# Per-head norm, rotation and key copies carried out in four rounds inside the projection of the second block

## What is computed

```python
x = swiglu_half_step(x, ...); h_ctx = swiglu_half_step(h_ctx, ...)
hx, hc = modulate(rms_norm(x, g1), ...), modulate(rms_norm(h_ctx, g1), ...)
px, pc = hx @ w_in, hc @ (w_in[:, Q_W:] if last else w_in)
qa, qb, ka, kb = rms_norm(heads(...), qk_norm_g[l, ...])   # each head of 64 by itself
qb, kb = apply_axial_rope(qb), apply_axial_rope(kb)        # tokens only, not the context
out = neighbourhood_attention(qa, ka, va, ...), windowed_gqa_attention(qb, kb, vb, ...)
x = x + gate * (out @ w_out)
x = swiglu_half_step(x, ...)
```

## Time and profile before

| | us |
|---|---|
| median of three runs | 2911.91 |
| lowest, highest of them | 2911.59, 2916.3 |
| the profiled execution | 2916.71 |
| its span, first to last instruction | 2914.9 |

### The profile page before, as it was taken

One profiled execution on the slowest core, in us unless ns is written; L12 is line 12 of the kernel. 1 busy time (PEld: TensorE's weight loads), 2 busy tenths in 40 slices (PEclk: granted clock), 3 DMA queues, 4 the chain that ended last, 5 costly groups with the idle time before them and its releaser, 6 DMA issues. The chain is left out here.

```text
span 2914.9 us, 39615 instructions
## 1 busy us (share of the span) xinstructions
PE 2634.1 (90%) x15379; PEld 2218.6 (76%) x15379; DVE 1756.6 (60%) x3178; ACT 1082.2 (37%) x2062; POOL 226.3 (8%) x169
## 2 busy tenths in 40 slices
PE   4768998798997899998999889999899998989899
PEld 4747997777997688886845668888688886856899
DVE  6567776558776666546648475554565444647654
ACT  2333543344443333223217333322333323326553
POOL 2000100000100210001000020000110000100110
PEclk8867998878998999999979999999999999889999
DMA  8923774824765244432710124433344433720453
GB/s 287 273 94 120 256 250 155 243 64 145 234 223 180 86 131 131 140 119 78 231 52 1 53 93 145 144 123 115 98 142 130 155 121 100 216 72 30 143 174 133
DMA packets 355667, 413.96 MB, mean 142 GB/s; under 512 B 25755, under 2 KB 292676, under 8 KB 355416
## 3 DMA queue, kind: packets, MB, share of 16 engines
q1 hardware_dynamic: 353326, 404.37, 43.6%
q0 software_dynamic: 800, 4.63, 0.5%
q10 hardware_dynamic: 1354, 2.43, 0.2%
HBM read 409.78 MB, written 5.27 MB: 142 GB/s over the span
## 5 line engine op out<-in xcount | busy, mean ns | idle before, releaser
L644 DVE TENSOR_TENSOR weight_lo<-raw_weights,weight_hi 128x512 fp32r<-128x512 f32 x1024 | 777.6, 766 | 936.3 <-ACT weight_hi L1180 925.7
L1180 ACT ACTIVATE weight_hi<-raw_weights 128x512 fp32r<-128x512 f32 x1024 | 633.3, 629 | 1332.1 <-PE bank L852 1188.0
L852 PE MATMUL bank<-H_hi,weight_hi 128*128 128x256 f32 (+1 forms) x2832 | 972.2, 343 | 118.6 <-POOL H_lo L810 80.5
L852 PE MATMUL bank<-H_lo,weight_hi 128*128 128x256 f32 (+1 forms) x2832 | 954.0, 337 | 0.0
L852 PE MATMUL bank<-H_hi,weight_lo 128*128 128x256 f32 (+1 forms) x2832 | 953.8, 337 | 0.0
L852 PEld LDWEIGHTS bank<-H_hi,weight_hi 128*128 128x128 f32 x2832 | 555.1, 196 | 197.0 <-issue 119.8
L852 PEld LDWEIGHTS bank<-H_hi,weight_lo 128*128 128x128 f32 x2832 | 555.4, 196 | 50.9
L852 PEld LDWEIGHTS bank<-H_lo,weight_hi 128*128 128x128 f32 x2832 | 556.9, 197 | 48.8 <-issue 0.5
L1475 DVE SCALAR_TENSOR_TENSOR ada_partial<-raw_weights,silu_c,ada_partial 128x512 f32<-128x512 f32 x616 | 441.6, 744 | 1.3 <-DVE ada_partial L1475 0.2
L852 PE MATMUL bank<-hidden_hi,weight_hi 128*128 128x256 f32 (+1 forms) x1056 | 360.0, 341 | 3.5 <-DVE weight_lo L644 3.5
L852 PE MATMUL bank<-hidden_hi,weight_lo 128*128 128x256 f32 (+1 forms) x1056 | 355.1, 336 | 0.0
(11 more groups left out here) (170 smaller groups left out, 2079.0 us busy)
## 6 DMA issues: line engine op xcount, KB each, us to landing
raw_weights<-in_w_ada_dram SPq DMA_DIRECT2D x120, 1024.0 KB, 5.3
raw_weights<-in_w_ffn_up_dram SPq DMA_DIRECT2D x88, 1024.0 KB, 5.2
raw_weights<-in_w_ffn_in_dram SPq DMA_DIRECT2D x44, 1024.0 KB, 5.3
raw_weights<-in_w_ffn_down_dram SPq DMA_DIRECT2D x32, 1024.0 KB, 5.1
raw_weights<-in_w_in_dram SPq DMA_DIRECT2D x18, 1024.0 KB, 8.1
raw_weights<-in_w_ffn_out_dram SPq DMA_DIRECT2D x16, 1024.0 KB, 7.7
raw_weights<-in_w_in_ab_dram SPq DMA_DIRECT2D x12, 1024.0 KB, 9.1
raw_weights<-in_w_in_cd_dram SPq DMA_DIRECT2D x12, 1024.0 KB, 8.2
```

Of the source, the lines that this page charges most:

```text
L644: eng.tensor_tensor(WL[:, p.g % SPLIT, 0:p.kt * CW].rearrange("p (t n) -> p t n", n=CW), raw_ap(ch.n, ch.kt, CW)[:, p.k0:p.k0 + p.kt, :], ...
L852: return pe.matmul(o, w, x, start=start, stop=stop, skip_group_check=True)
L1180: act.activation(WH[:, p.g % SPLIT, 0:p.kt * CW].rearrange("p (t n) -> p t n", n=CW), raw_ap(ch.n, ch.kt, CW)[:, p.k0:p.k0 + p.kt, :], ACT ...
```

## The change

The stage `qk_norm` is gone as a stage. Its work is done in four rounds inside the projection, at places that a table fixes: after piece j of item i. The items come in another order, kv first, then k, q and v. The head sums of a round go to four strips of 32 partitions of one bank, from squares that ScalarE now takes out of PSUM; the root and the reciprocal are made once per round; spreads, rotations and copies use two banks in turn. Only the first four items host ada chunks, and the four items of the output projection host one each. The loads of the attention stage come in five parts (34 of them), with five more (tables for the spreads, rotations and copies) ahead of the first. The forget columns are loaded and split in the setup, and have no chunk in the ring.

```diff
-    c["head_cols"] = (half[:, None] + 24 == np.arange(50)[None, :]).astype(f)
-    c["head_rows"] = (np.arange(26)[:, None] == (2 * np.arange(13)[:, None] + half[None, :]).reshape(1, -1)).astype(f)
+    c["head_sum"] = (half[:, None] == np.arange(32)[None, :] // 16).astype(f)
+    m = np.zeros((P, P), f)
+    for r in range(P):
+        if r % 16 == 0:
+            m[r] = half == r % 32 // 16
+    c["head_spread"] = m
...
+    FRAW = region("forget_raw", [P, KC, 8])
...
-    HEAD_ROWS = PR[0:26, :, :].rearrange("p j n -> p (j n)")
+    SPREAD = PR[:, 0, 0:P]
+    SQUARES = [T1[:, 0, :], T1[:, 1, :], T2[:, 0, :], T2[:, 1, :]]
...
+    ROUNDS = ((12, 8, 9), (10, 11, 4, 5), (6, 7, 0, 1), (2, 3))
+    ROUND_END = (3, 7, 11, 13)
+    QK_AT = {(2, 1): (("sums", 0),), (2, 2): (("recip", 0),),
+             (3, 1): (("spread", 12), ("spread", 8)), (3, 3): (("spread", 9),),
+             (4, 0): (("rope", 12),), (4, 1): (("sums", 1),), (4, 2): (("recip", 1),),
+             (5, 0): (("spread", 10), ("spread", 11)), (5, 1): (("spread", 4), ("spread", 5)),
+             (5, 3): (("dup", 0), ("dup", 1)),
+             (6, 0): (("rope", 4), ("rope", 5)), (6, 1): (("sums", 2),), (6, 2): (("recip", 2),),
+             (7, 0): (("neighbour", 0),), (7, 1): (("spread", 6), ("spread", 7)),
+             (7, 2): (("spread", 0), ("spread", 1)), (7, 3): (("sums", 3),),
+             (8, 0): (("recip", 3), ("rope", 6)), (8, 1): (("rope", 7),), (8, 2): (("spread", 2), ("spread", 3))}
...
+        all_hosted = len(ADA) if len(ADA) == sum(ADA_CHUNKS) else None
+        add("proj", hosted=all_hosted, n=n, groups=groups, ada=ada, gate=gate, half=False, hidden=False, first=first,
...
-                st.items.append(Item(what=what, chunk=chunk("f", view(w), 0, KC, c0, 8), grp=None, host=None, n=n))
+                st.items.append(Item(what=what, chunk=None, grp=None, host=None, n=n))
...
-            [(0, ("q", 0)), (256, ("q", 2)), (512, ("q", 4)), (768, ("q", 6)), (1024, ("k", 0)),
-             (1280, ("k", 2)), (1536, ("v", 0)), (1792, ("v", 256)), (2048, ("kv",))], n, 8, T if last else n, 2 + l)
-        add("bias", what="na", layer=l, take=bias_in.take(16 * 39))
-
-        tiles = [(i, 2 * T) for i in (12, 8, 9, 10, 11)] + [(i, T if last else n) for i in (4, 5, 6, 7, 0, 1, 2, 3)]
-        add("qk_norm", layer=l, items=tiles, sq=qn_sq.take(13), sums=qn_sums.take(13), mm=qn_mm.take(13),
-            root=qn_root.take(1), out=qn_out.take(13), rmm=rope_mm.take(7), ro=rope_out.take(7),
-            q_in=state["q_in"], bias_in=bias_in.total)
-        state["normed"] = (qn_out.total, rope_out.total)
+            [(2048, ("kv",)), (1024, ("k", 0)), (1280, ("k", 2)), (512, ("q", 4)), (768, ("q", 6)), (0, ("q", 0)),
+             (256, ("q", 2)), (1536, ("v", 0)), (1792, ("v", 256))], n, 4, T if last else n, 2 + l)
+        add("bias", what="na", layer=l, take=bias_in.take(16 * 34))
+        state["normed"] = qn_read.total
...
-        w_out(a["w_out_2"][l], n2, 2 + l, 5, False, 0)
+        w_out(a["w_out_2"][l], n2, 2 + l, 5, False, 4)
...
-                tiles += [(HEAD_ROWS[:, 0:13 * P], c["head_rows"]), (COS[:, :], c["cos"]), (SIN[:, :], c["sin"]),
-                          (NEIGH[:, :], c["neg_neighbour"]), (WINDOW[:, :, :].rearrange("p q k -> p (q k)"), c["neg_window"]),
-                          (dup[0][:, :], c["dup0"]), (dup[1][:, :], c["dup1"])]
+                if part == 0:
+                    for dst, src in ((SPREAD, c["head_spread"]), (COS[:, :], c["cos"]), (SIN[:, :], c["sin"]),
+                                     (dup[0][:, :], c["dup0"]), (dup[1][:, :], c["dup1"])):
+                        sp.dma_start(dst, src).then_inc(spread_in, 16)
+                tiles += [(NEIGH[:, :], c["neg_neighbour"]), (WINDOW[:, :, :].rearrange("p q k -> p (q k)"), c["neg_window"])]
...
+                    parts = 7 if s.layer < 2 else 5
+                    if 2 <= s.items.index(it) < 2 + parts:
+                        bias(after, s.items.index(it) - 2, parts)
...
+            pool.dma_start(FRAW[:, :, :], view(a["w_in_cd"][0])[:, :, 3 * D:3 * D + 8]).then_inc(fg_in, 16)
...
+                if hook:
+                    hook(i)
...
+        def qk_norm(s, i, j):
+            for what in QK_AT.get((i, j), ()):
+                kind, t = what
+                if kind == "sums":
+                    if t:
+                        pe.wait_ge(qn_root.sem, s.root + t)
+                    for k, tile in enumerate(ROUNDS[t]):
+                        pe.wait_ge(qn_sq.sem, s.sq + ROUND_END[t] - len(ROUNDS[t]) + k + 1)
+                        w = s.rows[tile]
+                        mm(B_STAT[32 * k:32 * k + 32, 0:w], head_sum[:, :], SQUARES[k][:, 0:w], True, True
+                           ).then_inc(qn_sums.sem, 1)
+                elif kind in ("spread", "rope", "dup"):
+                    pe.wait_ge(qn_read.sem, s.take[what] - 1)
+                    o = B_T[s.take[what] % 2]
+                    if kind == "spread":
+                        (r, k), w = place(t), s.rows[t]
+                        pe.wait_ge(spread_in, 16 * 5 * (s.layer - 1))
+                        pe.wait_ge(qn_rstd.sem, s.rstd + r + 1)
+                        rows = slice(32 * k, 32 * k + 32)
+                        ins = mm(o[:, 0:w], SPREAD[rows, :], RB[rows, 0:w], True, True)
+                    elif kind == "rope":
+                        pe.wait_ge(qn_read.sem, s.take["spread", t] + 1)
+                        ins = mm(o[:, 0:T], rotate[:, :], qk_tile(t)[:, 0:T], True, True)
+                    else:
+                        pe.wait_ge(qn_read.sem, s.take["rope", 12] + 1)
+                        ins = mm(o[:, :], dup[t][:, :], KB[:, 4, :], True, True)
+                    ins.then_inc(qn_mm.sem, 1)
...
-                    pe.wait_ge(forget_used, 1)
+                    pe.wait_ge(fg_lo, 1)
...
+            act.wait_ge(fg_in, 16)
+            act.activation(FH[:, :, :], FRAW[:, :, :], ACT.Copy).then_inc(fg_hi, 1)
...
+        def qk_squares(s, it):
+            pair = PAIR[it.grp.n % 2]
+            for j, t in enumerate(item_tiles(it)):
+                (r, k), w = place(t), s.rows[t]
+                if r:
+                    act.wait_ge(qn_sums.sem, s.sums + ROUND_END[r - 1])
+                act.activation(SQUARES[k][:, 0:w], pair[j][:, 0:w], ACT.Square).then_inc(qn_sq.sem, 1)
+        def qk_roots(s, i, j):
+            for kind, r in QK_AT.get((i, j), ()):
+                if kind == "sums":
+                    rows = slice(0, 32 * len(ROUNDS[r]))
+                    act.wait_ge(qn_sums.sem, s.sums + ROUND_END[r])
+                    if r:
+                        act.wait_ge(qn_mm.sem, s.mm["spread", ROUNDS[r - 1][-1]] + 1)
+                    act.activation(RB[rows, :], B_STAT[rows, :], ACT.Sqrt, bias=EPS[rows, 1:2], scale=1.0 / HD
+                                   ).then_inc(qn_root.sem, 1)
...
+            dve.wait_ge(fg_hi, 1)
+            dve.tensor_tensor(FL[:, :, :], FRAW[:, :, :], FH[:, :, :].bitcast(F32), ALU.subtract).then_inc(fg_lo, 1)
+            dve.wait_ge(fg_lo, 1)
...
+        def qk_norm(s, i, j):
+            for what in QK_AT.get((i, j), ()):
+                kind, t = what
+                if kind == "recip":
+                    rows = slice(0, 32 * len(ROUNDS[t]))
+                    dve.wait_ge(qn_root.sem, s.root + t + 1)
+                    dve.reciprocal(RB[rows, :], RB[rows, :]).then_inc(qn_rstd.sem, 1)
+                elif kind == "neighbour":
+                    dve.wait_ge(bias_in.sem, s.bias_in)
+                    blocks = BT[:, :].rearrange("p (b k) -> p b k", k=T)
+                    chain.link(dve.scalar_tensor_tensor(out=blocks, in0=blocks, scalar=-1.0,
+                                                        in1=NEIGH[:, None, :].broadcast_to([P, 16, T]), op0=ALU.mult,
+                                                        op1=ALU.add))
+                elif kind != "sums":
+                    o = B_T[s.take[what] % 2]
+                    dve.wait_ge(qn_mm.sem, s.mm[what] + 1)
+                    if kind == "spread":
+                        x, w = qk_tile(t), s.rows[t]
+                        k = 1 + 4 * (s.layer - 2) + (0 if t < 4 else 2 if t < 8 else 1 if t < 12 else 3)
+                        ins = dve.scalar_tensor_tensor(out=x[:, 0:w], in0=x[:, 0:w], scalar=E_COLS[:, k:k + 1],
+                                                       in1=o[:, 0:w], op0=ALU.mult, op1=ALU.mult)
+                    elif kind == "rope":
+                        x = qk_tile(t)[:, 0:T]
+                        dve.tensor_tensor(o[:, 0:T], o[:, 0:T], SIN[:, :], ALU.mult)
+                        chain.link(dve.tensor_tensor(x, x, COS[:, :], ALU.mult))
+                        ins = dve.tensor_tensor(x, x, o[:, 0:T], ALU.add)
+                    else:
+                        ins = dve.tensor_copy(KB[:, 5 + t, :], o[:, :])
+                    ins.then_inc(qn_read.sem, 1)
...
```

(36 more changed lines are left out.)

112 lines of the change are left out of this document (26 added, 86 removed).

## The result

The changed kernel takes **2865.2 us** (median of 4, 2863.3 to 2866.0) where the kernel before takes 2913.4 on the same chip: a ratio of **0.9834, 95% interval 0.9819 to 0.9850**. It is 48 us faster, where 79 were forecast; the range, 2815 to 2858, misses it.

The account below looks back on a forecast made before the run. TensorE, busy nine tenths of the span, was taken to bound the kernel. Pass A -32.6, B -35.6, forget -11.0 and setup +0.5 summed to -78.7 us, giving 2833 us on the median's scale; 8-in-10 range 2815 to 2858.

Parts of the forecast that it names:

- Serial stage (1): Behind each projection of the second block: the one-engine-at-a-time stage goes, -49.0 us in pass A, -41.1 in B.
- Matmuls in the projection (2): Sums, spreads, copies and rotations put on TensorE, small neighbours overlapping: 15.5 us added in pass A, 11.9 in B.
- the rival that they run one after the other: Small matmuls in the projection don't overlap: pass A pays 11.1 us more, B 7.9; 2849 us, chance 0.15.
- Waits (3): TensorE waits in the projection for VectorE's results: 2.4 us in pass A, 5.3 in B.
- The rival of a wait in all eight rounds: VectorE comes late and TensorE waits the 3.34 us reciprocal in every round: 2858 us, chance 0.10.
- kv first (4): kv moved under the modulation at the projection's start, mostly hidden: -2.9 us in pass A, -8.2 in B.
- The bound I wrote and didn't use: For moving kv to the projection's start: kv wholly at half clock, +10 us in each pass.
- The rival on the clock: Many short waits let TensorE's clock fall to 0.50 in both projections, costing 175 us: 3008 us, chance 0.03.
- Hosting (5): Ada chunks 4 to 7 moved to output projection: weight waits -5.1, closings -0.9 in B; output projection +1.4 A, +2.5 B.
- step 3: Its VectorE finding: 81 us of work in pass A's stage of over 100, with four ada chunks, so it doesn't bound.
- Forget (7): First block: without the forget columns' ring slot, TensorE's wait for forget_lo goes, -11.0 us, bounds -3 and -14.
- setup (8): A load of 1,024 short pieces in GpSimd's queue and two 64-column instructions: +0.5 us, bounds 0 and 5.

Follow-up runs that it names:

- experiment 4: Kernel before with one edit, kv moved to the head of the second block's projection items, serial stage kept: 2934.6 us, ratio 1.0060.
- experiment 2: Changed kernel, kv still first, with eight idle 512-column f32 matmuls filling TensorE's wait for the first H_lo tile: 2832.0 us, ratio 0.9714.
- experiment 10: Kernel before with only the forget columns done as in the changed kernel: 2904.2 us, ratio 0.9972.
- experiment 5: Kernel before with v (0) as the first item of the second block's projection: 2914.9 us beside 2917.7, single run.
- experiment 6: Changed kernel with kv's twelve 128-column token matmuls per H tile made six of 256 columns, output partly wrong: 2840.6 us beside 2920.4, single run.
- experiment 1: Changed kernel with its first two items exchanged, k (0, 1) first and kv second: 2845.7 us, ratio 0.9760.
- experiment 3: Changed kernel, wait ahead of the first H_lo tile filled with only four idle 512-column matmuls: 2872.3 us beside 2917.7, single run.
- experiment 7: Changed kernel, wait ahead of the first H_lo tile filled with 32 idle 128-column matmuls: 2830.0 us beside 2920.4, single run.

## Why the prediction was wrong, step by step

- **Serial stage (1).** Right: all 90 us are gone. Behind each projection the clock is still at 0.50 for 3.4 us, where I had forecast no such stretch; it is small.
- **Matmuls in the projection (2).** Right: 1.06 for three or four sums and 1.13 for a pair against 1.07; the rival that they run one after the other is refuted by the rows shown.
- **Waits (3).** Fewer than I had: 0.2 us in pass A for my 2.4, 2.8 in pass B for my 5.3, of which 2.0 for round 1's reciprocal at (5, 0), where I had 1.8. The rival of a wait in all eight rounds is refuted. What the step lacked is the price behind a wait: the 2.0 us one is followed by some 10 us at half clock, up to 5 us that I put at nothing.
- **kv first (4).** This is the step that failed. I wrote "At the half clock of that stretch kv falls behind for the first tiles and then runs 2.04 a tile", which took for granted that the clock comes back under kv as it did under q in pass A. It did not: kv's end came 37.9 us after the reciprocal in both passes, not 25.8, and k's first piece cost 4.0 us more in A, 2.9 in B. Booked: -2.9 and -8.2. By experiment 4 the edit alone costs 14.0 and 6.8 us instead, 16.9 and 15.0 worse than booked, beside the 15.9 and 19.4 by which the passes miss the forecast. The rest of B's is about the size of the half clock behind its wait.
- **The bound I wrote and didn't use.** The same step named "kv wholly at half clock (+10 each)". With it the sum is 2833 + 12.9 + 18.2 = 2864 us; 2865.2 were measured. But none of the rivals held this case, it got no chance, and the range stopped at 2858. That this sum lands within 2 us is in part luck, since other terms miss in both directions.
- **The rival on the clock.** It had the right mechanism in part: short waits in the projection letting the clock fall. In pass A the clock held at 1.00 after kv; in pass B it fell for 10 us, not for a whole projection. The evidence put against it doesn't hold either. In the q items of pass B the clock was at 1.00 in the window of the earlier trace rows, which ends at 2510, but right behind the next wait for weights it fell (timeline and table by stage of the kernel before):

```profile
2512.64 0.47 PE L852 MATMUL bank<-H_hi,weight_hi 128*128 128x512 f32 x1 [2.45 <-DVE weight_lo L644]
...
2514.00:2517.00 3.00, 3.00 (x9) 2.32 (x8) 3.00 (x5) 0.00 (x0) 0.00 (x0) 0.50 1.09 354
```

- **Hosting (5).** Wrong in sign in A, too small in B: I had +1.4 and -3.5; putting it back costs 6.9 and 7.9, so the edit gains that much in both. I counted DMA stalls and closings but not VectorE: the finding in step 3 that "it doesn't bound" used four hosted chunks, so it was this edit that made it true, and that was booked nowhere. The rest of the sum was too good by nearly as much (with eight chunks and the wait filled, pass A gains 27.3 us, where -49.0 + 17.9 - 2.9 is -34.0), so that the agreement of experiment 2 with the sums of both passes is in part two errors that cancel.
- **Forget (7) and setup (8).** Within the bounds: 8.2 us for both together by the timing of experiment 10. The stretch up to the first reciprocal shown moved with every execution (488 to 494 us, with and without the change), so its 5.7 us say nothing.
- **Open.** No part of the change that I costed lies between the stretch with the forget item and pass A, yet this took 662.4 to 662.9 us in the five kernels made from the one before and 657.4 to 662.4 in the seven made from the changed one, 2.8 us less on the mean. I did not find where. And why the clock comes back under one item and not under another is narrowed down (experiments 5 and 6), not settled.

## What to carry to other kernels

Where an item is moved to behind an idle stretch of TensorE, ask at which clock it will run and whether its own matmuls can bring the clock back; a busy share of 100% does not tell. Put an item there under which the trace has shown the clock come back, or fill the wait with idle matmuls, whose result nobody reads, up to the first real one. Look behind each short wait for the clock too, over all of the stage and not in one window of it. And where a known mechanism alone can carry a term to the end of its bounds, that end is a rival: give it a chance and let the range hold it, above all when the mechanism is in the rows already.

## What the runs showed of the hardware

- TensorE, "busy" 4.00 of 4.00 us in every window with fp32r matmuls of which four fifths were 128 columns wide, stayed at the granted clock 0.50 for all 31 us of kv, in six passes of three kernels. It kept 1.00 through the same item when it was there at its start (experiments 1 and 2).
- A 128-column fp32r matmul follows the last after 0.11 us at full clock, a 256-column one after 0.12, a 512-column one after 0.23; at half clock it is 0.21 for 128 and for 256 columns and 0.43 for 512. In f32 at full clock, 128 columns take 0.11 us a record and 512 take 0.43, two records a matmul.
- In 4.2 us of idleness the clock came down in both passes of experiment 3; behind the 2.27 us wait ahead of the last sum it came down in some passes and not in others (not in pass A of the run with narrow filling, but in its pass B).
- Behind the same wait of 1.99 us in pass B the clock was at 0.50 for some 10 us in the changed kernel and in experiments 1 and 3, for 3.4 us in experiment 2 and not at all in experiments 6 and 7.
